# Two transformer blocks on one core: split float32r products replaced by plain float32 products

## The reference

```python
proj = xn @ w_in[l]
...
h = h + rms_norm(mix @ w_out[l], ln_attn_post[l])
hn = rms_norm(h, ln_ffn_pre[l])
u = causal_dwconv(hn @ w_up[l], conv_w[l], conv_b[l])
gate, val = jnp.split(u, 2, axis=-1)
f = (jax.nn.gelu(gate, approximate=True) * val) @ w_down[l]
...
merged = g_a * (o_a @ w_branch_a[l]) + g_b * (o_b @ w_branch_b[l])
x = x + merged @ w_out[l]
h2 = rms_norm_2(x, norm2[l])
x = x + jnp.square(jax.nn.relu(h2 @ w_up[l])) @ w_down[l]
```

## Time and profile before

| | |
|---|---|
| median of 3 runs | 3332.52 us (3326.74 to 3333.29) |
| the profiled execution | 3327.89 us, of which the span is 3326.1 us |
| PE busy | 3082.3 us, 93% of the span |
| DVE, ACT, POOL busy | 1592.1, 969.9, 677.0 us |
| granted TensorE clock, mean | 0.975 of full speed |

### The profile page before, as it was taken

How to read it: one execution, slowest core, us unless ns; L and a number is a source line. 1 busy time by engine, 2 the same in 40 slices (tenths; PEclk the granted TensorE clock), 3 DMA queues, 4 the chain that set the end, 5 groups by cost and what they waited for, 6 DMA issues and landing times.

```text
span 3326.1 us, 48681 instructions
## 1 busy us (share of the span) xinstructions
PE 3082.3 (93%) x20334; PEld 2472.0 (74%) x20334; DVE 1592.1 (48%) x1898; ACT 969.9 (29%) x1434; POOL 677.0 (20%) x292
## 2 busy tenths in 40 slices
PE   7998988889799999999699999999799999999998
PEld 5876777777588788878468877666588877778776
DVE  3155667741744444444541134455544455454545
ACT  3144535632322122221331223333432211111112
POOL 2310121212522122221243410000022221222220
PEclk9998989989899999999899999999899999999999
DMA  4442330021411111111153534335454311111111
GB/s 167 150 127 79 114 115 24 25 67 51 135 56 45 44 38 57 48 46 38 39 167 126 185 94 145 121 97 156 160 170 127 129 36 51 50 50 50 44 33 62
DMA packets 233976, 292.69 MB, mean 88 GB/s; under 512 B 10057, under 2 KB 182226, under 8 KB 233818
## 3 DMA queue, kind: packets, MB, share of 16 engines
q1 hardware_dynamic: 218842, 243.22, 23.9%
q10 hardware_dynamic: 14976, 47.19, 3.7%
HBM read 209.86 MB, written 80.51 MB: 87 GB/s over the span
## 4 chain that ended last, share of the span: by engine, by line
PE 80%; DVE 10%; issue 5%; ACT 3%; DMA 1%; POOL 1%; SPq 0%; DVEq 0%; ACTq 0%; POOLq 0%
PE ps L359 58%; PE ps L1870 5%; PE ps L484 4%; PE ps L1320 3%; PE ps L1940 2%; PE ps L1921 2%; DVE cb L2447 1%; DVE xl L400 1%; PE ps L1898 1%; PE ps L1383 1%; DVE y L2357 1%; PE ps L1901 1%; POOL src L2250 1%; DMA vraw<-proj 1%; DVE cb L2396 1%
## 5 line engine op out<-in xcount | busy, mean ns | idle before, releaser
L336 POOL TENSOR_TENSOR wl<-wraw,wh 128x1024 fp32r<-128x1024 f32 x151 | 368.1, 2438 | 1675.7 <-ACT wh L331 1675.7
L359 PE MATMUL ps<-xh,wh 128*128 128x512 f32 x2192 | 685.6, 394 | 7.3 <-POOL xl L1164 2.3
L359 PE MATMUL ps<-xl,wh 128*128 128x512 f32 x2192 | 677.1, 390 | 0.0
L359 PE MATMUL ps<-xh,wl 128*128 128x512 f32 x2192 | 676.7, 390 | 0.0
L359 PEld LDWEIGHTS ps<-xh,wh 128*128 128x128 f32 x2192 | 412.0, 189 | 104.4 <-issue 7.3
L359 PEld LDWEIGHTS ps<-xl,wh 128*128 128x128 f32 x2192 | 412.9, 188 | 86.4
L359 PEld LDWEIGHTS ps<-xh,wl 128*128 128x128 f32 x2192 | 412.6, 188 | 86.3
L331 ACT ACTIVATE wh<-wraw 128x1024 fp32r<-128x1024 f32 x167 | 177.0, 1060 | 960.0 <-PE ps L359 886.3
L2357 DVE TENSOR_TENSOR y<-ps,y 128x1024 f32<-128x1024 f32 x208 | 252.4, 1223 | 254.2 <-PE ps L359 254.2
L2278 POOL TENSOR_TENSOR dl<-draw,dh 128x2048 fp32r<-128x2048 f32 x27 | 128.0, 4740 | 613.7 <-ACT dh L2274 613.7
L359 PE MATMUL ps<-dh,fh 128*128 128x512 f32 x512 | 160.2, 394 | 21.3 <-DVE y L2357 15.5
(11 more groups left out here) (319 smaller groups left out, 4486.7 us busy)
## 6 DMA issues: line engine op xcount, KB each, us to landing
wraw<-in_w_up SPq DMA_DIRECT2D x76, 512.0 KB, 3.9
wraw<-in_w_in SPq DMA_DIRECT2D x67, 512.0 KB, 4.4
draw<-in_w_down SPq DMA_DIRECT2D x27, 1024.0 KB, 5.1
residual<-src ACTq DMA_DIRECT2D x32, 512.0 KB, 4.9
proj<-stage SPq DMA_DIRECT2D x30, 512.0 KB, 3.0
qk_hi<-hs ACTq DMA_DIRECT2D x24, 512.0 KB, 2.7
qk_lo<-ls SPq DMA_DIRECT2D x24, 512.0 KB, 2.9
kh<-qk_hi SPq DMA_DIRECT2D x48, 256.0 KB, 7.0
```

The source lines that it names most:

```text
L336: nc.gpsimd.tensor_tensor(wl[:, s, :, :], wraw[:, s, :, :], wh[:, s, :, :].bitcast(F32), ALU.subtract).then_inc(w_lo, 1)
L359: mm = nc.tensor.matmul(ps[:, bank + h, :], w, x[:, h * HALF:(h + 1) * HALF], start=start and k == 0, stop=stop and k == 2)
```

## The change

All high and low tiles outside the attention scores go. `xh`, the weights, the down weights, the hidden values and the attention outputs are plain float32, and each `three_products` becomes one plain float32 product per half (`two_halves`): two matmul instructions per kt in place of six. The instructions that made the parts go, on ACT, POOL and DVE, with the DMAs of the low parts. The weights get four slots (`wt`), the down weights two (`dt`), and DMAs land in them directly; a load waits for the unit four before. In feed-forward 2, relu and square become one DVE instruction. The woven units are redistributed in matmul instructions of the new kind, so that units end at step ends; TAIL1 has 40 instructions (120 of the old ones) where it had 144 old ones, and the middle heads have 48 (144) where they had 132. Ahead of RWKV, unit 12 gets a tile of its own (`shifted_b`) and its shift comes later on DVE; the loads of `wa`, `gl` and r, k, v come earlier on SP; POOL's and DVE's orders in the first RWKV tile move.

```diff
+WEIGHTS = 4
-        xh = at("xh", 0, [P, KT, T], F32R)
-        xl = at("xl", 32, [P, KT, T], F32R)
-        wh = at("wh", 64, [P, 2, KT, P], F32R)
-        wl = at("wl", 72, [P, 2, KT, P], F32R)
-        wraw = at("wraw", 80, [P, 2, KT, P])
+        xh = at("xh", 0, [P, KT, T])
+        wt = at("wt", 64, [P, WEIGHTS, KT, P])
...
-        draw = at("draw", 104, [P, 2, D])
-        dh = at("dh", 88, [P, 2, D], F32R)
-        dl = at("dl", 96, [P, 2, D], F32R)
-        fh = at("fh", 148, [P, 2, 2, T], F32R)
-        fl = at("fl", 164, [P, 2, 2, T], F32R)
+        dt = at("dt", 88, [P, 2, 2, D])
+        ft = at("ft", 148, [P, 2, 2, T])
...
-        def split_hi(act, n, s, first=False):
-        def split_lo(pool, n, s, first=False):
...
+        def load_w(sp, n, source, slot=None):
+            if slot is None:
+                slot = n % WEIGHTS
+            if not isinstance(n, int) or n >= WEIGHTS:
+                sp.wait_ge(mm_done, n - WEIGHTS + 1)
+            sp.dma_start(wt[:, slot, :, :], source).then_inc(w_loaded[slot], 16)
...
             for kt in range(KT):
                 if before is not None:
                     before(kt)
                 if ready is not None:
-                    pe.wait_ge(x_lo, ready + kt + 1)
-                mm = three_products(2 * s, wh[:, s, kt, :], wl[:, s, kt, :], hi[:, kt, :], lo[:, kt, :],
-                                    kt == 0, kt == KT - 1)
+                    pe.wait_ge(x_hi, ready + kt + 1)
+                mm = two_halves(2 * s, wt[:, slot, kt, :], x[:, kt, :], kt == 0, kt == KT - 1)
             mm.then_inc(mm_done, 1)
-        def three_products(bank, w_hi_, w_lo_, x_hi_, x_lo_, start, stop):
-
-            for w, x, k in ((w_hi_, x_hi_, 0), (w_hi_, x_lo_, 1), (w_lo_, x_hi_, 2)):
-                for h in range(2):
-                    mm = nc.tensor.matmul(ps[:, bank + h, :], w, x[:, h * HALF:(h + 1) * HALF],
-                                          start=start and k == 0, stop=stop and k == 2)
+        def two_halves(bank, w, x, start, stop):
+
+            for h in range(2):
+                mm = nc.tensor.matmul(ps[:, bank + h, :], w, x[:, h * HALF:(h + 1) * HALF], start=start, stop=stop)
             return mm
...
-        def prep_dve(dve, r, q, gain, sums=False):
...
-        def hi_act(act, j):
-
-            out_dve.wait(act, "gate1", j)
-            out_act.done(fn_act(xh[:, j, :], y_mix[:, :], ACT.Copy), "hi")
...
-        THREE1 = [[12], [12], [12], [12], [12, 12], [12, 12], [12, 12], [12, 12]]
-        MIDDLE1 = [[9], [9], [9], [9], *THREE1[4:]]
-        LEAD1, TAIL1 = [12, 12], [24, 12, 12, 12, 12, 24, 48]
-        FILL1 = [[[6], [6], [6], [6], *THREE1[4:]], MIDDLE1, MIDDLE1, [*THREE1[:6], [6, 6], [6, 6]]]
+        THREE1 = [[4], [4], [4], [4], [4, 4], [4, 4], [4, 4], [4, 4]]
+        LEAD1, TAIL1 = [4, 4], [8, 4, 4, 4, 4, 16]
+        FILL1 = [[[2], [2], [2], [2], *THREE1[4:]], THREE1, THREE1, [*THREE1[:6], [2, 2], [2, 2]]]
...
+                elif u == 12:
+                    d1_pe.wait(dve, f"tv{HEADS1 - 1}1", 0)
+                    nc.vector.memset(shifted_b[:, 0:1], 0.0).then_inc(shift_b, 1)
...
             evac(12)
-            shift()
             for what in ("keys", "mixed", "decayed"):
                 prepare_dve(dve, 0, what)
             evac(13)
+            shift(1)
+            dve.wait_ge(stage_ready, 13)
+            scores_dve(dve, 0)
             shift()
...
-        TWO = [[4, 4], [4, 4], [4, 4], [4, 4], [4, 4, 4, 4], [0, 4, 4, 4], [4, 4, 4, 4], [5, 5, 5, 5]]
-        THREE = [[8, 8], [8, 8], [8, 8], [0, 8], [8, 8, 8, 8], [8, 0, 4, 4], [5, 5, 5, 5], [5, 5, 5, 5]]
-        LEAD = [6, 6]
+        TWO = [[1, 1], [1, 1], [1, 1], [1, 1], [1, 1, 1, 1], [1, 1, 1, 1], [2, 2, 2, 2], [2, 2, 2, 2]]
+        THREE = [[2, 2], [2, 2], [2, 2], [2, 2], [2, 2, 2, 2], [2, 2, 2, 2], [2, 2, 2, 2], [2, 2, 2, 2]]
+        LEAD = [2, 2]
...
                 for kt in range(2):
-                    mm = three_products(4 + 2 * (m % 2), dh[:, kt, m * P:(m + 1) * P], dl[:, kt, m * P:(m + 1) * P],
-                                        fh[:, par, kt, :], fl[:, par, kt, :], kt == 0, kt == 1)
+                    mm = two_halves(4 + 2 * (m % 2), dt[:, slot, kt, m * P:(m + 1) * P], ft[:, par, kt, :], kt == 0, kt == 1)
                 mm.then_inc(down_done, 1)
...
-                ff2_dve.done(nc.vector.tensor_scalar(cb[:, 1, :], cb[:, 0, :], 0.0, None, ALU.max), f"u{t}")
-                ff2_dve.wait(dve, f"u{t}", c)
-                ff2_dve.done(nc.vector.tensor_tensor(cb[:, 0, :], cb[:, 1, :], cb[:, 1, :], ALU.mult), f"r{t}")
+                dve.wait_ge(down_done, KT * (DOWN1 - 1 + c) + 1)
+                ff2_dve.done(nc.vector.scalar_tensor_tensor(out=ft[:, par, t, :], in0=cb[:, 0, :], scalar=0.0,
+                                                            in1=cb[:, 0, :], op0=ALU.max, op1=ALU.mult), f"r{t}")
                 if t == 0 and d is not None:
                     down_add(dve, d)
-                ff2_act.wait(dve, f"h{t}", c)
-                ff2_dve.wait(dve, f"r{t}", c)
-                ff2_dve.done(nc.vector.tensor_tensor(fl[:, par, t, :], cb[:, 0, :],
-                                                     fh[:, par, t, :].bitcast(F32), ALU.subtract), f"l{t}")
```

More of the change, by code:

```diff
@@ L319, in w_cols, with weights_ready, unit_products @@
             return w[0:rows, bass.ds(col0, P)].rearrange("(k p) c -> p k c", p=P)
[L321 to L324, removed]
[L326 to L343 removed]
+        def load_w(sp, n, source, slot=None):
[4 more added lines that the diff above has]
+            sp.dma_start(wt[:, slot, :, :], source).then_inc(w_loaded[slot], 16)
+        def weights_ready(pe, n, slot):
+            pe.wait_ge(w_loaded[slot], 16 // WEIGHTS * (n - slot) + 16)
+        def unit_products(pe, n, s, ready=None, first=False, x=None, before=None, slot=None):
+            x = xh if x is None else x
+            if slot is None:
+                slot = n % WEIGHTS
+            weights_ready(pe, n, slot)
             if not first:
@@ L1173, in rwkv_pool @@
                                 head_ident[:, :].unsqueeze(1).broadcast_to([P, NBLK, CHUNK]), ALU.add), f"I{hh}")
+            if j == 0:
+                for s in range(2):
+                    pool.wait_ge(stage_stored[s], STAGES1)
+                key_ends_pool(pool, 0)
             pre_dve.wait(pool, "pc", j)
@@ L1629, in d1_program_dve @@
                         output(b, n - 1)
-                    if n in (2, 3) and b:
-                        low(b - 1, n - 2)
                     if n + 1 < TT:
@@ L1701, in d1_reload @@
             for t in range(3):
-                load(t, 0, xh)
-            rw_pe.wait(sp, "YS", last)
-            for t in range(2):
-                load(t, 1, xl)
-            out_dve.wait(sp, "var", last)
-            for t in range(2, 4):
-                load(t, 1, xl)
+                load(t)
             out_pe.wait(sp, "tY1", last)
-            load(3, 0, xh)
+            load(3)
         PAIRS, FOX_PAIRS = 8, 4
@@ L2026, in a2_program_act @@
                         exps(b, n + 2)
-                    for part in range(2):
-                        for u in UNIT_ENDS.get((b, n, part), ()):
-                            split_hi(act, U_GATES + u + 2, (U_GATES + u) % 2)
                     if n == TT - 1 and b + 1 < PAIRS:
@@ L2123, in a2_program_dve @@
                         gate_evac(u)
-                    for u in lows:
-                        gate_lo(u)
-                    lows = []
-                    if n == 0 and b:
-                        low(b - 1, 1)
-                    if n == 5:
-                        low(b, 0)
                     for g in groups_of(b, n):
@@ L2134, in a2_program_dve @@
                         gate_evac(u)
-                    lows += [u for part in range(2) for u in UNIT_ENDS.get((b, n, part), ())]
                     if n == TT - 1 and b + 1 < PAIRS:
                         begin(b + 1)
-            low(PAIRS - 1, 1)
         def a2_loads(sp, b):
@@ L2195, in build_program @@
         added = sem("added")
-        d_loaded = sem("d_loaded")
-        d_hi = sem("d_hi")
-        d_lo = sem("d_lo")
+        d_loaded = [sem(f"d_loaded{s}") for s in range(2)]
         down_done = sem("down_done")
@@ L2696, in _ @@
                 rwkv_pool(pool, j)
-            for n in range(U_OUT + 2, U_UP + 2):
-                split_lo(pool, n, n % 2)
             post_norm_pool(pool, 0, 8, 16)
@@ L2753, in _ @@
             nc.scalar.activation(lam_dots[:, 0:2], lam_dots[:, 0:2], ACT.Exp).then_inc(lam_act, 1)
-            for s in range(2):
-                split_hi(act, s, s, first=True)
             for kt in range(KT):
@@ L2837, in _ @@
             stat_root_act(act, 5, 3)
-            ff2_act_chunk(act, 0, 0, first=True)
-            with act.Fori(0, DOWN2 // 2 - 1) as i:
-                for h in range(2):
-                    c = 2 * i + 1 + h
-                    ff2_act_chunk(act, c, (1 + h) % 2)
```

(3 more changed lines are left out.)

462 lines of the change are left out of this document (169 added, 293 removed).

## The result

The changed kernel takes 3815.45 us (median of 4 runs, 3807.09 to 3821.63) against 3329.63 us of the kernel before: 1.1465 times as long, 95% interval 1.1442 to 1.1488. The profiled execution has a span of 3812.9 us.

A forecast was written before the change was run, and what follows sets the result against it. PE, busy for 93% of the span, was taken as the bound. The terms sum as 3326.1 + 621 - 49 - 6 - 14 - 14 - 16 = 3848 us of span, plus 6 gives 3854 us; range 3770 to 3925.

The forecast's parts named there:

- The price: All 3536 products on PE: a plain one takes 0.855 us where three float32r ones take 0.6795, +621 us.
- Rival A: Products on PE: in a stream a plain one costs four float32r slots, 0.906 us, making 4034 us; chance 0.07.
- Chunks and ends of the feed-forwards: Feed-forwards: waits for DVE's add shrink, -49 us; waits ahead of the last down products shrink, -6 us.
- Norms and RWKV: Norms: DVE's low part goes and first units hide in idle time, -14 us; RWKV: shorter waits and chains, -14 us.
- The output projection: Behind RWKV's last tile: PE's 2.3 us wait for POOL's low part, with ACT's copy before it, goes, -3 us.
- Attentions: Both attentions: longer woven products cover more of PE's waits, -16 us, with ends at 0 and -69.
- The clock: Whole kernel: a granted clock at or above 0.975 was listed as a sign, with no term in the sum.
- B: Whole kernel: freeing DVE, ACT and POOL removes nearly all of PE's idle time, down to 3709 us; chance 0.06.
- C: Products on PE: one record pays for a whole plain product, 0.4275 us, so the time is near 2440; chance 0.02.
- D: Down loads in the feed-forwards: each of 27 makes PE wait some 5 us, making 3989 us; chance 0.03.
- E: Products on PE: plain tiles are multiplied like float32r, one record of 0.2265 us, well below 2500 us; chance 0.01.

The follow-up runs named there:

- e2: The changed kernel with three float32r products of the same high parts for each plain one, on fixed rounded weights: 3232.68 us, 0.9725 times before.
- e1: The kernel before with one plain product for each three float32r ones, all splits still made, second attention's portions as in the changed kernel: 3864.71 us, 1.1617 times before.
- e6: The changed kernel with the old order of the shifts of units 12 and 13 ahead of RWKV: 3811.27 us, 1.1466 times before.
- e5: The changed kernel with the old portions of woven products in the first attention: 3830.04 us, 1.1528 times before.
- e8: e4 plus the changed kernel's portions in the first attention, still with three products: 3266.02 us, 0.9825 times before.
- e4: The kernel before with relu and square as one DVE instruction, and output tile 0's add moved ahead of the convolution: 3285.44 us, 0.9871 times before.
- e7: The changed kernel with 11 ACT copies put back in the first attention, on tiles nobody needs: 3817.56 us, 1.1482 times before.
- e10: e8 plus the changed kernel's portions in the second attention, still with three products: 3257.93 us, 0.9787 times before.
- e9: The changed kernel with DVE's 16 weight subtractions put back in the second attention, on tiles nobody needs: 3817.72 us, 1.1468 times before.
- e3: The changed kernel with one float32r product for each plain one, on fixed rounded weights: 2137.85 us in a single run.

## Why the prediction was right, and where its terms were off

**The price.** The step that carries the sum held: two records for a plain product, at a distance taken from one pair in a norm. The pair gave 0.4275 us a record, the stream 0.4292. The timeline of PEld in feed-forward 2 of the changed kernel, nine steps in 3.87 us, which answers the earlier trace rows:

```profile
3100.04 0.19 PEld L342 LDWEIGHTS ps<-dt,ft 128*128 128x128 f32 x1 [0.24 <-issue]
...
3103.91 0.19 PEld L342 LDWEIGHTS ps<-xh,wt 128*128 128x128 f32 x1 [0.24 <-issue]
```

The term was sized at +621 and measured +632.6. Rival A (0.906 us, four old slots) is off by 0.048 us a product: a float32r product costs 12 ns more than half of a plain record, and a plain product doesn't pay these four times. The Trainium skill ("FP8 and Floating Point Precision", "TensorE Precision Notes") gives a true float32 product four passes through the array. They fit the two records if each record makes two; no run here shows the passes themselves.

**Chunks and ends of the feed-forwards.** -55 forecast, and by the table -28.8 and -25.6: -54.4. (The -49 of the chunks is 48 by its factors as printed.) I left 0.6 us a chunk in feed-forward 1; it is 0.37. The stall is now this, against the earlier trace rows:

```profile
1087.08 2.43 DVE L2245 TENSOR_TENSOR y<-ps,y 128x1024 f32<-128x1024 f32 x2
1087.23 0.19 PEld L342 LDWEIGHTS ps<-ft,dt 128*128 128x128 f32 x1 [0.24 <-issue]
1088.35 0.30 PEld L342 LDWEIGHTS ps<-ft,dt 128*128 128x128 f32 x2 [0.93 <-DVE y L2245]
```

DVE comes to the add 5.5 us behind the evacuation (at 1081.57), where it was 5.9 (1008.63 to 1014.51): the freed engines give only 0.4 us here, as the waits of e2 say too. The row of 2.43 us is two adds; the first ends at 1088.30 and PE's load follows at 1088.35. PE had started the last record of tile 1 at 1087.66, starts the first of tile 2 at 1088.36 and the second at 1088.89: 1.23 us for two records of 0.43, which is the 0.37 lost. e1 and e2 together show that both reasons given were real in feed-forward 1 (42.1 to 19.4 by length, to 28.7 by freeing the engines), and that in feed-forward 2 either alone takes most (28.5 to 9.0, or to 3.5).

At the end of feed-forward 1 the wait is 7.1 us where it was 9.9, so 2.8 went and 2.5 were forecast to go:

```profile
1805.98 2.90 PE L342 MATMUL ps<-ft,dt 128*128 128x512 f32 x3 [7.15 <-issue]
```

In feed-forward 2 it is 2.7 where it was 5.8: 3.1 went, and 3 were forecast to.

**Norms and RWKV.** -14 and -14 forecast, -17.7 and -13.0 measured (RWKV with the rest of the woven units and the output projection). Within RWKV the parts were wrong. From the turn of the last attention output to the first scores the stretch fell from 14.4 to 7.3 us beyond its products, near the 8 of the forecast, but the two steps behind the scores got 4.0 us longer, so 3.1 are left. The reason was not the forecast one: e1, with the old order and all the splits, has 6.5 in the same stretch, and e6 shows the moved shift gave nothing. Over all of RWKV, with the woven units ahead of it, PE is idle for 40 us in both kernels, and the granted clock is 0.95 in the kernel before and 0.98 in the changed one (0.03 x 287 = 9 us at most, enough for the 6.3 us of the table's row). The output projection gave 6.7 where 3 were forecast. I had read DVE's 43 busy of 55 us as the pace, but PE's woven products, 34 us of them, fill the same stretch.

**Attentions: the term that was mis-sized.** -16 forecast, -57.5 measured (-32.4, -20.5 and -4.6 in the last heads). I had priced the longer portions only. In the first attention e1 gives some 13 for length. The larger part is the new distribution of the portions, which I had listed in the change and did not price: 16.7 us of the stage by e5 against the changed kernel, 23.0 by e8 against e4. Its row stood in the earlier trace rows, the 10.9 us of waits for `shifted`. I had its idle time in the stretch of the earlier trace rows, but not asked what ended it. Some two thirds of what it gives are PE's idle time, the wait and others; most of the rest is clock, 0.97 in e4 and 1.00 in e8. e7 shows that ACT's freed copies give 1.5 us at most in this stage.

In the second attention the split of the 20.5 us is not fully shown. The 12.9 of e1 hold length and the new portions together, and e10 gives the portions 3 to 10. The other 7.6, from e1 to the changed kernel, have the same portions and length. e9 shows that DVE's freed subtractions are not their cause; ACT's freed copies, the low parts that PE no longer waits for and the four weight slots weren't tried apart. At the old length the same step, from e10 to e2, is worth 7.7 us (218.1 to 210.4).

So the sum missed by +12 for the price and -47 for the rest, which is the 35 us between 3848 and 3812.9. The two misses partly cancel, which is luck. The clock had no term: it stood among the signs, at or above 0.975, and its rise to 0.986 is part of what the stages gave back.

**The other rivals.** B (nearly all of PE's idle time goes) didn't come: 94 us of it went and 150 remain. The waits for squares in the norms are still here, 35.2 us where they were 42.4:

```profile
PE ps L358 <- ACT sq L350: 35.2, 9, 14.7
```

C needed a product below 0.7075 us and got 0.8583. D (loads in the way) left no wait of PE for `wt` or `dt` in the trace; even in e3, at a quarter of the price, PE waits 16.8 us for `wt` and not at all for `dt`. E fell with the 7072 records.

## What to carry to other kernels

A float32 product on TensorE is dearer here than three float32r products of the same shape (0.858 against 0.680 us for 128x128 by 128x512), so where PE sets the time, as here, dropping the split costs more than the rest of the change gives back: 633 us against 146. To price an instruction that a kernel doesn't have yet, look for a small use of it elsewhere in the same trace, count its records against the code, and take the distance between starts. When work is woven between other work, price where its units end as well as how long its portions are: in the first attention that was worth 15 to 23 us by itself, about a third of it through the granted clock. The adds and portions of the change can be had without its price: e10, with three products, is 2.1% faster than the kernel before.

## What was not expected of the hardware

A plain product's record took 0.4275 us in a pair and 0.4292 us in a stream, with a granted clock of 1.00 in both. The weight loads stand at 0.19 us in either kernel and each of the two records has its own, yet in the stream of plain products the load engine is idle for 0.24 us of every 0.43: so loads don't pace the plain stream, while a float32r product at 0.2265 us leaves its load of 0.19 only some 0.04 us of room.
